# Gate and up products of both layers' experts: plain fp32 instead of three products of rounded parts

## The reference, cut to what matters

```python
def expert_choice_ffn(h, w_router, w_gate, w_up, w_down):
    cap = CAPACITY_FACTOR * T // N_EXPERTS           # 64 of 512 tokens, 32 of 256
    aff = softmax(h @ w_router)                      # [T, 16]
    g, idx = lax.top_k(swapaxes(aff, 1, 2), cap)     # each expert picks its tokens
    xe = h[idx]                                      # 16 experts x cap x 1024
    a = einsum('becd,edf->becf', xe, w_gate)         # 1024 x 1024 per expert
    u = einsum('becd,edf->becf', xe, w_up)
    y = einsum('becf,efd->becd', silu(a) * u, w_down) * g[..., None]
    return zeros((T, D)).at[idx].add(y)
```

## Time and profile before

| | |
|---|---|
| median of three runs | 2790.18 us (2782.98 to 2791.01) |
| profiled execution, first to last instruction (its span) | 2786.7 us |
| TensorE busy | 2494.8 us, 90% of the span |
| VectorE busy | 1798.3 us, 65% |
| ScalarE busy | 1205.5 us, 43% |
| GpSimd busy | 293.8 us, 11% |
| chain that ended last | TensorE 74%, VectorE 12%, ScalarE 7% |

### The profile page before, as it was taken

One profiled execution on the slowest core, in us unless ns is written; L12 is line 12 of the kernel. 1 busy time (PEld: TensorE's weight loads), 2 busy tenths in 40 slices (PEclk: granted clock), 3 DMA queues, 4 the chain that ended last, 5 costly groups with the idle time before them and its releaser, 6 DMA issues.

```text
span 2786.7 us, 28893 instructions
## 1 busy us (share of the span) xinstructions
PE 2494.8 (90%) x10367; PEld 1484.9 (53%) x10367; DVE 1798.3 (65%) x2962; ACT 1205.5 (43%) x2121; POOL 293.8 (11%) x349
## 2 busy tenths in 40 slices
PE   8899979998958999999997699799894999999996
PEld 1255467887535555555554444688743444444442
DVE  1278567776356777777775232677626877878875
ACT  0012156554226555555553221555423555555552
POOL 0000011000112111111110100000011011110110
PEclk9999988998978999999999799899896999999998
DMA  7955330001137998998997200300025899999993
GB/s 275 340 181 159 82 81 1 1 1 50 72 119 247 318 332 304 318 321 315 323 319 266 52 0 0 81 1 1 25 101 184 322 345 335 339 339 339 349 334 104
DMA packets 257908, 534.74 MB, mean 192 GB/s; under 512 B 24854, under 2 KB 57798, under 8 KB 257768
## 3 DMA queue, kind: packets, MB, share of 16 engines
q1 hardware_dynamic: 251624, 511.93, 52.4%
q0 software_dynamic: 6144, 20.98, 3.1%
HBM read 505.87 MB, written 27.00 MB: 191 GB/s over the span
## 4 chain that ended last, share of the span: by engine, by line
PE 74%; DVE 12%; ACT 7%; issue 4%; SPq 1%; DMA 1%; POOL 0%; POOLq 0%; ACTq 0%; DVEq 0%
PE ps L972 16%; PE ps L791 13%; PE ps L948 7%; PE ps L950 7%; PE ps L949 7%; PE ps L893 5%; PE ps L851 5%; PE ps L828 4%; ACT arena L1176 4%; DVE w_l L1593 3%; PE ps L842 3%; PE ps L730 2%; DVE nmx L1456 2%; PE ps L819 1%; ACT arena L1210 1%
## 5 line engine op out<-in xcount | busy, mean ns | idle before, releaser
L1593 DVE TENSOR_TENSOR w_l<-arena,w_h 128x1024 fp32r<-128x1024 f32 x512 | 657.6, 1305 | 284.9 <-ACT w_h L1198 275.5
L1198 ACT ACTIVATE w_h<-arena 128x1024 fp32r<-128x1024 f32 x512 | 533.1, 1067 | 421.9 <-PE ps L950 384.5
L948 PE MATMUL ps<-w_h,xeT_h 128*96 128x512 f32 (+1 forms) x1024 | 428.0, 418 | 64.3 <-DVE w_l L1593 53.3
L972 PE MATMUL ps<-arena 128*96 128x512 f32 (+1 forms) x1024 | 451.5, 594 | 1.4 <-DVE arena L1613 1.4
L950 PE MATMUL ps<-w_h,xeT_l 128*96 128x512 f32 (+1 forms) x1024 | 412.3, 403 | 0.0
L949 PE MATMUL ps<-w_l,xeT_h 128*96 128x512 f32 (+1 forms) x1024 | 411.3, 402 | 0.0
L791 PE MATMUL ps<-arena 128*128 128x512 f32 (+1 forms) x960 | 396.8, 572 | 7.2 <-issue 4.1
L972 PEld LDWEIGHTS ps<-arena 128*96 128x96 f32 (+1 forms) x1024 | 150.8, 150 | 269.0 <-issue 264.6
L791 PEld LDWEIGHTS ps<-arena 128*128 128x128 f32 x960 | 182.6, 193 | 198.7 <-issue 191.4
L948 PEld LDWEIGHTS ps<-w_h,xeT_h 128*96 128x96 f32 (+1 forms) x1024 | 156.5, 153 | 170.2 <-issue 65.6
L1105 ACT ACTIVATE arena<-ps,nmx 128x768 f32<-128x768 f32 (+3 forms) x200 | 158.2, 791 | 182.6 <-DVE nmx L1460 137.7
(11 more groups left out here) (171 smaller groups left out, 2469.2 us busy)
## 6 DMA issues: line engine op xcount, KB each, us to landing
arena<-in_w_gate SPq DMA_DIRECT2D x64, 2048.0 KB, 13.9
arena<-in_w_up SPq DMA_DIRECT2D x64, 2048.0 KB, 11.0
arena<-in_w_down SPq DMA_DIRECT2D x64, 2048.0 KB, 9.5
arena<-in_w_ada SPq DMA_DIRECT2D x12, 2048.0 KB, 10.1
arena<-in_w_ada SPq DMA_DIRECT2D x48, 512.0 KB, 3.8
arena<-in_w_in SPq DMA_DIRECT2D x10, 2048.0 KB, 15.4
arena<-in_w_out SPq DMA_DIRECT2D x16, 512.0 KB, 5.9
y<-arena SPq DMA_DIRECT2D x10, 512.0 KB, 5.3
```

What stands on the lines that cost most here:

```text
L948: pe.matmul(out, hi, wh, start=(c == 0), stop=False)
L972: mm = pe.matmul(pb(4 + h)[0:M, :], hsT[:, 4 * half + c, 0:M], w[:, c, 512 * h:512 * h + 512], start=(half == 0 and c == 0), stop=(half == ...
L1198: act.activation(w_hi[piece % PIECES].rearrange("p c n -> p (c n)"), unit[SLOT[part]][:, D * (q % 4):D * (q % 4) + D], ACT.Copy).then_inc( ...
L1593: dve.tensor_tensor(lo, unit[SLOT[part]][:, D * (q % 4):D * (q % 4) + D], hi.bitcast(F32), ALU.subtract).then_inc(s_lo, 1)
```

## The change

Gate and up go the way `down` already goes: one plain fp32 product per chunk, eight in a call, from the loaded unit and from the full `xeT`. `high_pieces`, `low_pieces`, `split_xe` and their buffers and semaphores are removed; `xeT` now has two buffers. TensorE itself waits for the unit's load (`s_w`) and for `xeT` (`s_ec`), and `s_pr` counts calls (4 an expert) instead of pieces (16). SyncE waits for `s_pr` ahead of the next load into a gate or up slot.

```diff
-        xeT = at(136, [KC, 96])
-        xeT_hi, xeT_lo = ([at(139 + 6 * s + 3 * k, ...) for s in range(2)] for k in range(2))
+        xeT = [at(139 + 3 * s, [KC, 96]) for s in range(2)]
...
-                            sp.wait_ge(s_lo, 16 * E + 4 * part + 4)
+                            sp.wait_ge(s_pr, 4 * E + part + 1)
...
-                def split_xe(e):
-                    ...
-                    link(pool.tensor_copy(hi, full))
-                    pool.tensor_tensor(lo, full, hi.bitcast(F32), ALU.subtract).then_inc(s_xs, 1)
...
-                    for q in range(4):
-                        piece = 16 * E + 4 * (2 * half + part) + q
-                        pe.wait_ge(s_lo, piece + 1)
-                        for j in range(2):
-                            c = 2 * q + j
-                            ...
-                            pe.matmul(out, hi, wh, start=(c == 0), stop=False)
-                            pe.matmul(out, hi, wl, start=False, stop=False)
-                            mm = pe.matmul(out, lo, wh, start=False, stop=(c == KC - 1))
-                        mm.then_inc(s_pr, 1)
+                    slot = SLOT[2 * half + part]
+                    pe.wait_ge(s_w[slot], 16 * (E + 1))
+                    w = unit[slot].rearrange("p (c n) -> p c n", n=512)
+                    for c in range(KC):
+                        mm = pe.matmul(out, xeT[e % 2][:, c, 0:M], w[:, c, :], start=(c == 0), stop=(c == KC - 1))
+                    mm.then_inc(s_pr, 1)
...
-                    pe.wait_ge(s_xs, NE * l + e + 1)
+                    pe.wait_ge(s_ec, 2 * (NE * l + e + 1))
                     gate_up(e, 0, 0)
...
-                    if e:
-                        act.wait_ge(s_xs, E)
+                    if e >= 2:
+                        act.wait_ge(s_pr, 4 * (E - 1))
...
                 for e in range(NE):
-                    high_pieces(e, 4, 11)
                     exp_gate(e, 0)
-                    high_pieces(e, 11, 12)
                     if e:
                         store_y(e - 1)
                     if e + 1 < NE:
                         modulate_xe(e + 1)
-                    high_pieces(e, 12, 16)
-                    high_pieces(e + 1, 0, 3)
                     exp_gate(e, 1)
-                    high_pieces(e + 1, 3, 4)
...
-                    low_pieces(e, 4, 8)
                     if e:
                         store_hidden(e - 1, 1)
-                    low_pieces(e, 8, 11)
                     hidden(e, 0)
-                    low_pieces(e, 11, 16)
                     store_hidden(e, 0)
-                    low_pieces(e + 1, 0, 3)
                     hidden(e, 1)
-                    low_pieces(e + 1, 3, 4)
```

More of the change, by code:

```diff
@@ L268, in hybrid_dit @@
         unit = [at(16 * s, [4096]) for s in range(RING)]
-        PIECES = 4
-        w_hi, w_lo = ([at(96 + 8 * s + 4 * k, [2, 512], rounded=f"w_{'hl'[k]}{s}") for s in range(PIECES)] for k in range(2))
         xe = [at(128 + 4 * s, [D], parts=96) for s in range(2)]
-        xeT = at(136, [KC, 96])
-        xeT_hi, xeT_lo = ([at(139 + 6 * s + 3 * k, [KC, 96], rounded=f"xeT_{'hl'[k]}{s}") for s in range(2)] for k in range(2))
+        xeT = [at(139 + 3 * s, [KC, 96]) for s in range(2)]
         hs = at(151, [D], parts=96)
@@ L383, in hybrid_dit @@
         s_wf = sem("s_wf")
-        s_hi = sem("s_hi")
-        s_lo = sem("s_lo")
         s_pr = sem("s_pr")
@@ L390, in hybrid_dit @@
         s_ec = sem("s_ec")
-        s_xs = sem("s_xs")
         s_eg = sem("s_eg")
@@ L662, in gather @@
                                             ).then_inc(s_g[e % 2], 16)
-                def split_xe(e):
[L666 to L670, removed]
-                    link(pool.tensor_copy(hi, full))
-                    pool.tensor_tensor(lo, full, hi.bitcast(F32), ALU.subtract).then_inc(s_xs, 1)
                 gather(0)
                 gather(1)
-                split_xe(0)
                 for e in range(NE):
@@ L680, in _ @@
                         gather(e + 2)
-                    if e + 1 < NE:
-                        split_xe(e + 1)
                     pool.wait_ge(s_yc, E + 1)
@@ L940, in gate_up @@
                     out = pb(2 * half + part)[0:M, :]
-                    for q in range(4):
-                        piece = 16 * E + 4 * (2 * half + part) + q
-                        pe.wait_ge(s_lo, piece + 1)
-                        for j in range(2):
-                            c = 2 * q + j
-                            hi, lo = xeT_hi[e % 2][:, c, 0:M], xeT_lo[e % 2][:, c, 0:M]
-                            wh, wl = w_hi[piece % PIECES][:, j, :], w_lo[piece % PIECES][:, j, :]
-                            pe.matmul(out, hi, wh, start=(c == 0), stop=False)
-                            pe.matmul(out, hi, wl, start=False, stop=False)
-                            mm = pe.matmul(out, lo, wh, start=False, stop=(c == KC - 1))
-                        mm.then_inc(s_pr, 1)
+                    slot = SLOT[2 * half + part]
[4 more added lines that the diff above has]
+                    mm.then_inc(s_pr, 1)
                 def turn_hs(e, half):
@@ L1175, in modulate_xe @@
                                 if a < b:
-                                    ins = act.activation(xeT[:, c, a:b],
+                                    ins = act.activation(xeT[e % 2][:, c, a:b],
                                                          pb(6 + half)[:, P * (c % 4) + a:P * (c % 4) + b], ACT.Identity,
@@ L1183, in exp_gate @@
                     E = NE * l + e
-                    act.wait_ge(s_pr, 16 * E + 8 * half + 8)
+                    act.wait_ge(s_pr, 4 * E + 2 * half + 2)
                     if E:
@@ L1187, in exp_gate @@
                     act.activation(sg[0:M, half, :], pb(2 * half)[0:M, :], ACT.Exp, scale=-1.0).then_inc(s_eg, 1)
[L1189 to L1199, removed]
                 act.wait_ge(s_tc, 2 * (l + 1))
-                high_pieces(0, 0, 4)
                 modulate_xe(0)
@@ L1584, in _ @@
                 dve.tensor_copy(idxT[0:M, 0:NE], pb(5)[0:M, 0:NE]).then_inc(s_tc, 1)
[L1586 to L1594, removed]
                 def hidden(e, half):
@@ L1614, in store_hidden @@
                                     pb(6 + half).rearrange("p (c n) -> p c n", n=P)[:, :, 0:M]).then_inc(s_hsc, 1)
-                low_pieces(0, 0, 4)
                 for e in range(NE):
-                    low_pieces(e, 4, 8)
                     if e:
                         store_hidden(e - 1, 1)
-                    low_pieces(e, 8, 11)
                     hidden(e, 0)
-                    low_pieces(e, 11, 16)
                     store_hidden(e, 0)
-                    low_pieces(e + 1, 0, 3)
                     hidden(e, 1)
-                    low_pieces(e + 1, 3, 4)
                 store_hidden(NE - 1, 1)
-                dve.wait_ge(s_pr, 16 * NE * (l + 1))
+                dve.wait_ge(s_pr, 4 * NE * (l + 1))
                 for k in range(2):
```

## The result

The changed kernel takes 2862.26 us (median; 2859.78 to 2865.99), the kernel before 2787.54 us in the same comparison: a ratio of 1.0265, 95% interval 1.0247 to 1.0283. It is slower by 75 us where 81 were forecast. The profiled execution has a span of 2859.7 us, 73.0 more than before.

A forecast was written before the change was run, and what follows sets the result against it. TensorE was taken as the bound in layer 1, with slack in layer 0 from waits for low pieces. First experts and bulks, -1.4 + 8.8 + 0 + 73.8 = +81.2 us on the 2790.2 us median, gave 2871 us; range 2855 to 2897.

The forecast's parts named there:

- Cost of a call: TensorE's gate and up calls: from 5.60 to 6.87 us in layer 0, from 5.68 to 7.01 in layer 1.
- sum by rows: TensorE work added over 15 experts, from call times: 76 us in layer 0 and 80 us in layer 1.
- count of passes: Skill's rule for gate and up products: four passes for true fp32 against three reduced ones, adding 221 us.
- Fewer records: Rival, gate and up calls: a plain product is one 0.43 us record, a call 3.44 us; 2626 us total; chance 2%.
- dearer calls: Rival, gate and up calls: adjacent plain calls cost 7.34 and 7.41 us, +52 us, 2923 us total; chance 4%.
- The size of layer 1's call: Layer 1's gate and up calls: 7.01 us, taken from that layer's own `down` row; bounds 6.87 to 7.01.
- the bulk: Each layer's 15 experts after the first: +8.8 us to 635.2 in layer 0, +73.8 to 651.6 in layer 1.
- The turns: TensorE's transposes in layer 0: hidden rows 0.28 us (0.39 in layer 1), `turn_xe` 0.61 (0.64), durations kept.
- Covers and loads at nothing: Hidden rows, modulation and later slot releases cost nothing: tightest cover fits by about 1 us, loads have 36 us.
- 70 us that the splits cause.: Layer 0's expert stage: 45 us of waits for low pieces plus 25 us of lower clock; layer 1 about 3.
- the clock: Rival, both expert stages: lower clock comes back with plain products, 0.96, +50 us, 2921 us total; chance 4%.
- First experts: Start of each stage: TensorE starts 2.8 and 2.1 us earlier, lower clock takes 2.2 and 2.8; net -1.4 and 0.

The follow-up runs named there:

- rounded_fixed: Changed kernel's order and waits, but three rounded products a chunk from four pieces rounded once a layer, other splits and low parts left out; 2702.9 us, 0.9694 to before.
- late_loads: Changed kernel with each load of a gate or up unit issued two calls later; 2871.9 us, ratio 1.0300 to the kernel before.
- Late_split_before: Kernel before with one more wait on GpSimd, which splits the next expert's rows only after VectorE's last low piece; 2742.1 us, ratio 0.9817.
- reorder: Kernel before with the second half of ScalarE's modulation of the next expert's rows moved behind high pieces 12 to 15; 2712.6 us, ratio 0.9740.
- cols96: Changed kernel with gate and up of layer 1 run with 96 columns of weights like layer 0; 2873.6 us, ratio 1.0304 to the kernel before.
- all96: Changed kernel with all of TensorE's work in layer 1's stage in layer 0's forms (96 rows or columns); 2861.4 us, ratio 1.0233 to the kernel before.

## Why the prediction was right

**What bounds the kernel.** Right: TensorE in both layers, with layer 0's slack in its waits for low pieces and the clock behind them.

**Cost of a call.** Right in kind (16 records, two a product; 6.87 us in layer 0, to the hundredth) and the direction with it; rounded_fixed gives the difference without any wait: 77.9 + 73.4 = 151.3 us over the 30 experts, where the sum by rows had 156. The 221 us over 32 experts that the prediction worked out from a count of passes don't come out. "Fewer records" and "dearer calls" are out by the rows of starts.

**The size of layer 1's call was the step that was off.** "I take each layer's own row: ... 7.01 in layer 1". A `down` of the kernel before had a rounded call or a transpose on either side. With plain neighbours of its own form a call costs 6.87, between two turns 7.02, 6.94 in the mean: 0.41 us an expert, 6.2 of the 6.5 us by which the bulk missed. The prediction held the right value as a bound (6.87 to 7.01) but took the own row for the nearest without asking what stood next to it.

**The turns.** 0.33 and 0.66 us in layer 0 instead of 0.28 and 0.61, now that only plain products stand next to them (0.28 and 0.61 again in rounded_fixed): 15 x 2 x 0.05 + 14 x 0.05 = 2.2 us, the whole miss of layer 0's bulk (+10.9 for +8.8).

**Covers and loads at nothing.** Right: no wait of TensorE in either bulk, the hidden rows and the modulation fit, the loads have over 14 us to spare. "Nothing is queued behind SyncE's wait but the next loads" overlooked the last expert, whose last `w_down` unit stands behind such waits with no next expert to cover it; late_loads paid for that, the change didn't.

**"70 us that the splits cause."** Right in size as something that goes with the change: layer 0's bulk before was 626.5 - 559.4 = 67.1 us above TensorE's own time, 45.2 of it waits (in layer 1 577.7 - 571.7 = 6.0, where 3 were put). So 151.3 us of dearer products less 73.1 given back make the 78.2 of the two bulks. The rival "the clock" is out: 1.00 in both. The cause was told too simply. Late_split_before and reorder show that it was the place of two instructions: GpSimd's subtraction beside VectorE's first low piece, and half of ScalarE's modulation ahead of the high pieces. The splits as such cost nothing in either bulk: reorder keeps them all and has no wait.

**First experts.** -0.5 and -1.4 us for -1.4 and 0. TensorE starts as much earlier as foreseen (4.7 and 2.5 us behind the start of ScalarE's modulation, 7.5 and 4.6 before). What the lower clock takes is read from the first two calls:

```profile
839.67 16.85 PE L926 MATMUL ps<-arena 128*96 128x512 f32 x32 [4.14 <-ACT arena L1152]
856.35 0.82 PE L912 MATMUL ps<-ident,arena 96*128 96x96 f32 x8
...
2138.93 15.73 PE L926 MATMUL ps<-arena 128*64 128x512 f32 x32 [2.20 <-ACT arena L1152]
2154.59 0.71 PE L912 MATMUL ps<-ident,arena 64*128 64x64 f32 x8
```

16.68 us for 2 x 6.87 and 15.66 for 6.87 + 6.96 are 2.9 and 1.8 us lost, where 2.2 and 2.8 were put. The turns' 0.1 us in layer 0 and the cheaper calls' 0.4 in layer 1 are the rest.

## What to carry to other kernels

Work taken off engines that run beside the bound engine gives back only the waits that it caused, so look at those waits one by one before removing the work: here moving half of ScalarE's modulation behind four pieces gave back 74 us with the work kept, and removing it all at TensorE's expense lost 75. For the price of an instruction read a row that also has the neighbours it will have, not only its own form. And where a wait's releaser is late, compare its duration with the median of its group: 2.88 against 1.23 us pointed to a third engine.

## What the runs showed of the hardware

A product of rounded operands costs 0.23 us and a plain fp32 one 0.86, so three rounded products are 1.2 to 1.3 us a call of eight chunks cheaper than one plain product.

A VectorE subtraction of two SBUF operands beside a GpSimd subtraction that began with it or 0.01 us earlier is longer by nearly the other's length: 2.88 us instead of 1.23 beside 1.81 in the kernel before, 2.92 beside 1.84 in reorder. The profile shows no wait for it; it is in the duration.

Where one of two neighbouring matmuls has 64 rows or columns and the other has another form (64 against 96 columns, 64-row transposes against 128-row products, rounded against plain at 64 columns), a plain call of 16 records costs 0.05 to 0.17 us more than 6.87. Between 96-column products and 96-row transposes there is no such cost. The Trainium skill, TensorEngine Tiling (Array Packing), section Key Properties, says that a change of the tiling mode drains TensorE. The rows of cols96 and all96 agree with such a cost and put these numbers to it; which of the forms here are different tiling modes no row shows.

In reorder the transfers of layer 0 have a share of 1.00 at 357 GB/s. The Trainium skill, Perfetto Trace Analysis, section Engine Utilization, gives 358 GB/s as memory bandwidth of a core, and says under Roofline that a core alone in its pair can draw more; 6 us at 387 GB/s in the kernel before agree with that. TensorE waits for no load in reorder. How much faster TensorE could go before it did no run shows.
